# Expert units in pairs over 512 columns, the lower one with its weights straight from the ring

## The reference

```python
g_idx = jnp.argmax(g_logits, axis=-1)                      # 1 of 4 groups
top_vals, top_idx = lax.top_k(e_in, TOP_K)                 # 2 of its 8 experts
for gi in range(N_EXPERT_GROUPS):
    hg = jnp.einsum('nd,edf->nef', xt, w_eg[gi])           # 1024 -> 256, gate
    hu = jnp.einsum('nd,edf->nef', xt, w_eu[gi])           # 1024 -> 256, up
    h = jax.nn.silu(hg) * hu * combine[:, gi, :, None]
    y = y + jnp.einsum('nef,efd->nd', h, w_ed[gi])         # 256 -> 1024, down
```

## Time and profile before

| | us |
|---|---|
| median of 3 runs | 1335.88 |
| lowest, highest | 1333.59, 1340.38 |
| the profiled execution, its own time | 1345.06 |
| its span, first to last instruction | 1343.3 |
| end of the last expert's matmul (start 1284.26 and 2.86) | 1287.1 |

### The profile page before, as it was taken

One profiled execution on the slowest core, in us unless ns is written; L12 is line 12 of the kernel. 1 busy time (PEld: TensorE's weight loads), 2 busy tenths in 40 slices (PEclk: granted clock), 3 DMA queues, 4 the chain that ended last, 5 costly groups with the idle time before them and its releaser, 6 DMA issues.

```text
span 1343.3 us, 25378 instructions
## 1 busy us (share of the span) xinstructions
PE 1166.9 (87%) x9960; PEld 723.4 (54%) x9960; DVE 781.9 (58%) x1330; ACT 381.5 (28%) x668; POOL 257.5 (19%) x321
## 2 busy tenths in 40 slices
PE   4999999999998689999789899953999989999920
PEld 3455555555556578888784455432555545454500
DVE  4277799862314688888733132247555546555546
ACT  4100011011213245555420111111344434443421
POOL 5000000000002223232200000002343434342310
PEclk9899999999999799999969899965999999999965
DMA  7311111010000011110251211073999998775046
GB/s 203 98 32 32 32 39 47 16 37 20 0 0 5 14 21 17 17 17 15 46 171 36 94 63 55 32 281 121 393 383 365 414 423 339 309 289 187 32 185 237
DMA packets 101209, 171.80 MB, mean 128 GB/s; under 512 B 48156, under 2 KB 72595, under 8 KB 91840
## 3 DMA queue, kind: packets, MB, share of 16 engines
q1 hardware_dynamic: 93215, 152.70, 31.8%
q0 software_dynamic: 7904, 17.84, 3.6%
HBM read 153.83 MB, written 26.11 MB: 134 GB/s over the span
## 4 chain that ended last, share of the span: by engine, by line
PE 67%; DVE 12%; DMA 11%; issue 5%; ACT 2%; SPq 1%; POOL 1%; DVEq 1%; POOLq 0%; ACTq 0%
PE ps L1396 26%; PE ps L1700 9%; PE ps L1809 7%; DMA late<-xn_rows,g_idx 6%; PE ps L1423 4%; PE ps L1831 4%; PE ps L1444 2%; DMA arena<-in_w_exp_down_dram 2%; DMA arena<-y_rows 2%; DVE arena L2102 1%; PE ps L1796 1%; PE ps L1728 1%; PE ps L1432 1%; DMA arena<-in_x_prompt_dram 1%; DVE arena L2105 1%
## 5 line engine op out<-in xcount | busy, mean ns | idle before, releaser
L1396 PE MATMUL ps<-arena 128*128 128x512 f32 (+1 forms) x1056 | 348.9, 492 | 0.6 <-ACT arena L881 0.6
L1396 PEld LDWEIGHTS ps<-arena 128*128 128x128 f32 x1056 | 176.3, 193 | 174.4 <-issue 173.6
L1809 PE MATMUL ps<-arena 128*64 128x256 f32 x1664 | 201.8, 385 | 4.9 <-DVE arena L2480 4.9
L1928 DVE SCALAR_TENSOR_TENSOR arena<-arena,cw 128x1024 f32<-128x1024 f32 x240 | 168.2, 778 | 0.4
L1809 PEld LDWEIGHTS ps<-arena 128*64 128x64 f32 x1664 | 117.7, 138 | 85.0 <-issue 35.7
L2480 DVE COPY arena<-arena 128x4096 f32 x52 | 119.5, 2299 | 74.9 <-issue 52.6
L1700 PE MATMUL ps<-arena 128*128 128x512 f32 (+1 forms) x288 | 128.9, 603 | 0.0
L1209 ACT ACTIVATE arena<-arena 128x2048 f32 x52 | 99.4, 1912 | 64.8 <-PE ps L1831 40.9
L1423 PE MATMUL ps<-arena 64*64 64x64 f32 x2864 | 98.9, 222 | 13.8 <-DVE arena L2114 9.8
L1831 PE MATMUL ps<-arena 128*64 128x512 f32 x416 | 103.2, 617 | 8.3 <-DVE arena L2496 5.0
L1423 PEld LDWEIGHTS ps<-arena 64*64 64x64 f32 x2864 | 92.2, 138 | 18.8 <-DVE arena L2114 10.9
(11 more groups left out here) (298 smaller groups left out, 1476.5 us busy)
## 6 DMA issues: line engine op xcount, KB each, us to landing
arena<-in_w_exp_gate_dram SPq DMA_DIRECT2D x32, 1024.0 KB, 8.1
arena<-in_w_exp_up_dram SPq DMA_DIRECT2D x32, 1024.0 KB, 10.8
arena<-in_w_exp_down_dram SPq DMA_DIRECT2D x32, 1024.0 KB, 10.4
arena<-in_w_in_dram SPq DMA_DIRECT2D x22, 512.0 KB, 4.0
arena<-in_x_prompt_dram SPq DMA_DIRECT2D x16, 512.0 KB, 4.2
arena<-y_rows SPq DMA_DIRECT2D x8, 1024.0 KB, 5.8
arena<-in_w_out_dram SPq DMA_DIRECT2D x2, 2048.0 KB, 9.7
xn_rows<-arena SPq DMA_DIRECT2D x8, 512.0 KB, 2.9
```

What stands on the lines that cost most here:

```text
L1396: ins = pe.matmul(pr[:, n0:n1], win[q % 6][:, c, :], xnT[:, c, n0:n1], start=(c == 0), stop=(c == DC - 1))
L1809: ins = pe.matmul(banks(j % 2)[HS * h:HS * h + HS, 0:2 * P], xgT[(j // 2) % 2][:, c, tok], wgu[j % 2][:, :, c, h * P:(h + 1) * P], start=( ...
L1928: dve.scalar_tensor_tensor(out=dst, in0=src, scalar=w, in1=dst, op0=ALU.mult, op1=ALU.add).then_inc(conv_tap, 1)
```

## The change

The loop goes by pairs instead of units. gate_up makes for each chunk two matmuls of 512 columns side by side, the lower 64 rows of the array's output for the lower unit, the upper 64 for the upper one. The lower unit's matmuls read gate, up and down weights from the ring, at an address that PE takes from a register (slot_of); only the upper unit's weights are copied, so DVE and ACT make one weight copy per pair. Sigmoid, products, hidden transposes, their copy and the output copies are made once per pair at twice the width, gathers and scatters once per pair.

SP's loop is reordered. A slot is free for the gate and up weights of e when PE has finished gate_up of the last unit of e-4 (gu_psum, which goes up by two at the end of a pair), and for down weights when the down projection is done (yd_psum, likewise). The arrival of gate and up weights and that of down weights are announced apart (gu_here, wd_here). dve_step(g) issues copy_gate_up(g+2) after the products of pair g+1.

The tables are changed too: counts are rounded to units by arithmetic instead of by comparisons with 16 thresholds, the tables of expert and slot are made with one unit to a partition and turned into a row by PE (two small matmuls), `turns_ready` is set before the row tables are, and the softmax's weights are computed after them.

```diff
--- before.py
+++ after.py
-UT = 4
-HS = P // 2
+NQ = 2
+HS = P // NQ
 RW = 4
 NUNIT = NE + (N * TOPK - NE) // HS
-NUP = -(-NUNIT // UT) * UT
+NUP = -(-NUNIT // (2 * NQ)) * 2 * NQ
+NGR = NUP // NQ
+ROUND = 12582912.0
...
-            def expert_arrived(e):
+            def gate_up_arrived(e):
                 sp.wait_ge(wgu_in[e % RW], wgu_0[e % RW] + 32 * (e // RW + 1))
+                sp.sem_inc(gu_here, 1)
+            def down_arrived(e):
                 sp.wait_ge(wd_in[e % RW], wd_0[e % RW] + 16 * (e // RW + 1))
-                sp.sem_inc(expert_here, 1)
+                sp.sem_inc(wd_here, 1)
+            def units_through(e):
+                return sp.value_load(expert_ends[0:1, e:e + 1], min_val=1, max_val=NUP)
...
-            expert_arrived(0)
+            gate_up_arrived(0)
+            gate_up_arrived(1)
+            down_arrived(0)
             sp.wait_ge(turns_ready, 1)
-            tail_sp = sp.value_load(last_turn[0:1, 0:1], min_val=NE // UT - 2, max_val=NUP // UT - 2)
-            for e in range(RW, NE + 1):
+            tail_sp = sp.value_load(last_turn[0:1, 0:1], min_val=NE // (2 * NQ) - 2, max_val=NGR // 2 - 2)
+            for e in range(RW, NE + 3):
                 if e < NE:
-                    units_done = sp.value_load(expert_ends[0:1, e - RW:e - RW + 1], min_val=1, max_val=NUP)
-                    sp.wait_ge(gu_copied, units_done)
+                    sp.wait_ge(gu_psum, units_through(e - RW))
                     load_gate_up(e)
-                    expert_arrived(e - RW + 1)
-                if e > RW:
-                    units_done = sp.value_load(expert_ends[0:1, e - RW - 1:e - RW], min_val=1, max_val=NUP)
-                    sp.wait_ge(down_copied, units_done)
+                if e - 2 < NE:
+                    gate_up_arrived(e - 2)
+                if RW <= e - 1 < NE:
+                    sp.wait_ge(yd_psum, units_through(e - 1 - RW))
                     load_down(e - 1)
-            for e in range(NE - RW + 1, NE):
-                expert_arrived(e)
-            all_units = tail_sp * UT + 2 * UT
-            scattered = tail_sp * 16 + 32
-            sp.wait_ge(yd_psum, all_units)
+                down_arrived(e - 3)
...
+            def scatter(g, b):
+                pool.wait_ge(ye_act, g + 1)
+                pool.wait_ge(ye_dve, g + 1)
...
+            def pool_step(turn, b, left):
+                g = 2 * turn + b
+                if left >= 4:
+                    pool.wait_ge(xT_psum, 2 * NT + g + 3)
+                    gather(g + 4, b)
+                scatter(g, b)
...
+            def copy_down(g):
+                u = NQ * g + 1
+                need = act.value_load(unit_need[0:1, bass.ds(u, 1)], min_val=1, max_val=NE)
+                slot = act.value_load(unit_slot[0:1, bass.ds(u, 1)], min_val=0, max_val=RW - 1)
+                act.wait_ge(yd_psum, NQ * g)
+                act.wait_ge(wd_here, need)
...
+            def act_step(turn, b, left):
+                g = 2 * turn + b
                 if left >= 1:
-                    sigmoid(u + 1, j + 1)
-                if j % 2 == 0:
-                    if left >= 5:
-                        copy_xg(2 * turn + j // 2 + 2, (j // 2) % 2)
-                    act.wait_ge(yd_psum, u + 1)
-                    act.wait_ge(ye_out[j], 16 * turn)
-                    act.activation(ye[j], banks(5), ACT.Copy).then_inc(ye_act, 1)
+                    sigmoid(g + 1, 1 - b)
+                if left >= 2:
+                    copy_xg(g + 2, b)
+                act.wait_ge(yd_psum, NQ * g + NQ)
+                act.wait_ge(ye_out[b], 16 * turn)
+                act.activation(ye[b][:, 0:512], banks(5), ACT.Copy).then_inc(ye_act, 1)
                 if left >= 1:
-                    copy_down(u + 1)
+                    copy_down(g + 1)
...
+            def slot_of(g):
+                return pe.value_load(unit_slot[0:1, bass.ds(NQ * g, 1)], min_val=0, max_val=RW - 1)
+            def gate_up(g, b, chunks, slot):
                 if 0 in chunks:
-                    if j % 2 == 0:
-                        pe.wait_ge(xT_act, 2 * NT + pair + 1)
-                        pe.wait_ge(xT_dve, 2 * NT + pair + 1)
-                    pe.wait_ge(gu_copied, u + 1)
+                    pe.wait_ge(xT_act, 2 * NT + g + 1)
+                    pe.wait_ge(xT_dve, 2 * NT + g + 1)
+                    pe.wait_ge(gu_copied, g + 1)
                 for c in chunks:
-                    for h in range(2):
-                        ins = pe.matmul(banks(j % 2)[HS * h:HS * h + HS, 0:2 * P], xgT[(j // 2) % 2][:, c, tok],
-                                        wgu[j % 2][:, :, c, h * P:(h + 1) * P], start=(c == 0), stop=(c == DC - 1))
+                    pe.matmul(banks(b)[0:HS, :], xgT[b][:, c, 0:HS],
+                              wring_gu[:, bass.ds(slot, 1), 0:2, c, :].rearrange("p a w f -> p (a w) f"),
+                              start=(c == 0), stop=(c == DC - 1))
+                    ins = pe.matmul(banks(b)[HS:P, :], xgT[b][:, c, HS:P], wgu[b][:, :, c, :], start=(c == 0),
+                                    stop=(c == DC - 1))
                 if DC - 1 in chunks:
-                    ins.then_inc(gu_psum, 1)
-            def pe_step(turn, j, left):
-                u = UT * turn + j
-                next_pair = 2 * turn + (j + 1) // 2
+                    ins.then_inc(gu_psum, NQ)
+            def pe_step(turn, b, left):
+                g = 2 * turn + b
                 if left >= 1:
-                    gate_up(u + 1, next_pair, j + 1, range(0, 5))
-                pe.wait_ge(hx_done, u + 1)
-                pe.transpose(banks(4)[:, (j % 2) * P:(j % 2 + 1) * P], gu, ident[:, :]).then_inc(ht_psum, 1)
+                    slot = slot_of(g + 1)
+                    gate_up(g + 1, 1 - b, range(0, 4), slot)
+                pe.wait_ge(hx_done, g + 1)
+                for c in range(2):
+                    ins = pe.transpose(banks(4)[:, c * P:(c + 1) * P], gu[:, c * P:(c + 1) * P], ident[:, :])
+                ins.then_inc(ht_psum, 1)
                 if left >= 1:
-                    gate_up(u + 1, next_pair, j + 1, range(5, DC))
-                if j % 2 == 0 and left >= 5:
-                    transpose_rows(2 * turn + j // 2 + 2, turn, j // 2 + 2)
-                pe.wait_ge(ht_done, u + 1)
-                pe.wait_ge((ye_act, ye_dve)[j % 2], 2 * turn + j // 2)
-                pe.wait_ge(down_copied, u + 1)
-                for c in range(2):
-                    for h in range(2):
-                        ins = pe.matmul(banks(5 + j % 2)[HS * h:HS * h + HS, :], hT[:, HS * c:HS * c + HS],
-                                        wd[:, c, h * 512:h * 512 + 512], start=(c == 0), stop=(c == 1))
-                ins.then_inc(yd_psum, 1)
+                    gate_up(g + 1, 1 - b, range(4, DC), slot)
+                slot = slot_of(g)
+                if left >= 2:
+                    transpose_rows(g + 2, turn + 1, b)
+                pe.wait_ge(ht_done, g + 1)
+                pe.wait_ge(ye_act, g)
+                pe.wait_ge(ye_dve, g)
+                pe.wait_ge(down_copied, g + 1)
+                for half in range(2):
+                    for c in range(2):
+                        n0 = 2 * DC * F + c * D + half * 512
+                        pe.matmul(banks(5 + half)[0:HS, :], hT[:, c, 0:HS],
+                                  wring[:, bass.ds(slot, 1), n0:n0 + 512].rearrange("p a n -> p (a n)"),
+                                  start=(c == 0), stop=(c == 1))
+                        ins = pe.matmul(banks(5 + half)[HS:P, :], hT[:, c, HS:P], wd[:, c, half * 512:half * 512 + 512],
+                                        start=(c == 0), stop=(c == 1))
+                ins.then_inc(yd_psum, NQ)
...
-            dve.wait_ge(softmax_done, 1)
-            RED(r_pg, r_gd, ALU.add)
-            dve.wait_ge(softmax_done, 2)
-            TS(r_den, r_ex, 1.0, None, ALU.add)
-            TT(r_den, r_den, r_pg, ALU.mult)
-            link(dve.reciprocal(w_k[:, 0, :], r_den))
-            TT(w_k[:, 1, :], w_k[:, 0, :], r_ex, ALU.mult)
...
+            def whole_units(out, v, shift):
+                TS(out, v, 1.0 / HS, shift - 0.5 + 0.5 / HS, ALU.mult, ALU.add)
+                TS(out, out, ROUND, None, ALU.add)
+                TS(out, out, -ROUND, None, ALU.add)
...
+            TS(r_le, upto, r_pid, None, ALU.is_le)
+            RED(r_te, r_le, ALU.add)
+            TS(r_te, r_te, float(NE - 1), None, ALU.min)
+            TS(r_fc, r_thr, r_te, None, ALU.is_le)
+            RED(r_fl, r_fc, ALU.add)
+            link(dve.scalar_tensor_tensor(out=r_col[:, 0:1], in0=r_fl, scalar=-float(RW), in1=r_te, op0=ALU.mult,
+                                          op1=ALU.add))
+            dve.tensor_scalar(r_col[:, 1:2], r_te, 1.0, None, ALU.add).then_inc(cum_done, 1)
...
+                for i in range(NT):
+                    ins = dve.tensor_scalar(r_os[k][:, i, :], r_iots, slot[:, i:i + 1], r_val[:, i:i + 1], ALU.is_equal,
```

(103 more changed lines are left out.)

200 lines of the change are left out of this document (70 added, 130 removed).

## The result

The changed kernel takes **1386.36 us** (median of 4 runs, 1385.35 to 1393.52) against 1337.03 for the kernel before in 4 runs beside it (1333.59 to 1340.38): ratio **1.038**, interval 1.034 to 1.043, slower. The forecast was 1379 in a range of 1346 to 1406. The profiled execution took 1385.48, its span is 1383.7. Between the medians lie 49.3 us where the forecast had 43.

The account below looks back on a forecast made before the run. Bound: DVE's 13.0 us chain against PE's 11.9, plus SP's late announcements. 947.2 + 24 x 13.0 + 36 + 9 x 1.6 = 1309.6; PE ends at 1329, 42 later; scatter 1; 43 on 1335.88 gives 1379 us, range 1346 to 1406.

Parts of the forecast that it names:

- The sign and the mechanism: Loop by pairs: slower, as PE waits for DVE's weight copy and SP's late announcements; 0.85 chance of slower.
- the sum: Whole kernel: PE ends 42 us later, the last scatter adds 1, so 43 us slower.
- PE's stream: PE's own work on a pair: 11.9 us, 0.4 less than before, taken alone worth 10 us.
- Rival 3: PE's wide matmuls save all the rows allow, 0.4 us for each of 26 pairs: 1369 us; chance 0.02.
- DVE's chain: From gate_up through sigmoid, products, row copy, register reads and weight copy to the next gate_up: 13.0 us a cycle.
- The eight long cycles: Pairs 2, 4, 6, 9 to 13: SP's late announcement adds 3.6 us to five, 6.1 to three, 36 in all.
- the clock: PE after 4.7 or 7.2 us idle: lower clock costs 1.4 to 1.9 us a time, 1.6 taken, nine times.
- Tables and start: Before the loop: gate_up(0) starts near 932.0 instead of 939.93, bounds 0 and 10 us gained; gate_up(1) at 947.2.
- 1 (announcements don't hold the copy): SP's announcements don't hold DVE's weight copy, only the 13.0 us cycle is left: 1325 us; chance 0.15.
- 2 (registers on PE): PE pays for its register reads and addresses, 1.0 us in each of 26 pairs: 1405 us; chance 0.12.
- 4 (a quicker SP, or a clock that holds): Long cycles exist but cost less: 1365 us if the clock holds, 1347 with half of the 36 gone; chance 0.11.
- the weights' transfer is hidden: DMA in pairs of one-unit experts: 17.9 us a pair, within cycles of 19.1 and more, so no added time.

Follow-up runs that it names:

- the first experiment: Changed kernel with SP announcing gate and up weights one iteration earlier, before the wait for the down projection: 1350.96 us, ratio 1.009.
- three small edits: In the changed kernel: gate and up announced one iteration earlier, weight copy before the products, down load one iteration later; together 1330.98 us, ratio 0.994.
- the kernel with both orders: Changed kernel with gate and up announced one iteration earlier, DVE's weight copy before the products, down load one iteration later: 1330.98 us, ratio 0.994.

## Why the prediction held, and where it was off

**The sign and the mechanism held.** By positions of the two profiled executions: the part ahead of the tables -7.3 (no part of the change), tables -9.8, from gate_up(0) to PE's end 1326.7 - 922.8 = 403.9 against 347.2, +56.7, and behind it +0.8: sum 40.4, as their own times differ. Without the first it is 47.7 where the sum said 43. The 4.7 are the balance of misses both ways: from gate_up(1) to gate_up(25) it is 369.9 instead of 362.4, +7.5; the tables -1.9; from gate_up(0) to gate_up(1) +0.4; from gate_up(25) to PE's end 18.4 instead of 19.5, -1.1; the last scatter -0.2.

**PE's stream.** Forecast 11.9, measured 12.0 where nothing disturbs it. Rival 3 needed it shorter still. 0.34 a pair is gained, no more than the rows' 0.4. The Trainium skill, "TensorEngine Tiling (Array Packing)", section Instruction Overhead, gives each matmul some 60 cycles of overhead. Added to every matmul, which is how the prediction made its estimate from that page, it would have the stream 0.8 shorter than the forecast, 11.1; the trace, with 12.0, disagrees. The prediction's use of it had a fault of its own: the 0.214 us for 512 columns was measured, so any overhead is in the 11.9 already. The section adds that a matmul of one column takes as long as one of 60; read as such a floor it says nothing of 256 or 512 columns, and no run here tests it.

**DVE's chain.** 13.0 forecast, 12.83 to 13.13 measured. Its interpolated steps were right: sigmoid of 256 columns 0.384 (0.38), products 0.424 (0.42). That it is the bound is shown by the copy's place: ahead of the products the cycle is 12.0.

**The eight long cycles** are those named, pairs 2, 4, 6, 9 to 13. They sum to 160.2 us where the forecast has 5 x 18.2 + 3 x 20.7 = 153.1. The idle times ahead of the eight gate_ups were right (46.2 in all against 45.1). The term that was most **mis-sized is the clock**: from gate_up to the hidden transposes they take 4.97 to 6.58 us instead of 3.58, 2.0 more on average where the step said 1.6, at most 3.0 where it said 1.9; that is 3.5 of the 7.1 us. Another 2.5 is PE's step, 12.2 in this kernel without idle time and clock, where 11.9 was taken; the last 1.1 is the idle time.

**Tables and start.** 9.8 gained, 7.9 forecast, both within the bounds. gate_up(1) starts 15.6 after gate_up(0), 15.2 forecast; the announcement for it did come with the second SP iteration (934.38), but the products and the row copy end it, as the step had them in this order.

**Rivals.** 1 (announcements don't hold the copy) fell with the first experiment, and its price was near: that kernel's three long cycles hold 57.5 - 3 x 13.0 = 18.5 us, and without them it would be at 1332, where the rival said 1325. 2 (registers on PE) is refuted for the reads by the doubled reads; matmuls with a register address can cost no more than the 0.1 between the 11.9, put together from rows without one, and the 12.0 measured. 4 (a quicker SP, or a clock that holds) went the other way. That the weights' transfer is hidden is shown for the changed kernel, by half of their bytes and by SP's rows; once SP's order is mended it is hidden no longer.

The clock wasn't tried by itself: no edit was found that leaves PE idle and keeps its clock.

## What to carry over

When a copy that ran ahead becomes the last thing before its consumer, write down the new ring (consumer, producer's queue, consumer) and sum it: where it is longer than the consumer's own work it is the new cycle, however much work the change saves. Follow each announcement back through the queue that makes it: here a wait for the consumer's own last step stood one or two iterations ahead of it, and with the queue's order on DVE this cost 55 us, which three small edits gave back. What that queue itself waited for tells order from rate: 120.5 us for the consumer's last step and none for a DMA here, 4.3 and 98 after the edits. And order a queue so that what may be late stands behind what is ready, unless it is never late.

## What the hardware showed that was not expected

- The same idle time cost PE quite different amounts afterwards: behind 4.6 to 4.9 us idle the first half of gate_up took 4.97, 5.04, 5.20, 5.28 and 6.43 us (3.58 at the upper level), behind 7.4 to 7.8 us idle 5.27, 6.22 and 6.58.
- PE's reads of a register cost nothing that could be measured (ratio 0.9945 with 51 more reads, 0.9936 without), where two reads on DVE show as 0.83 to 0.95 us of idle time ahead of its copy. Matmuls whose address comes from a register (L1815) take as long as those beside them with a fixed one (L1818): 209.1 and 209.2 us for 416 records each.
- The copy of 4096 columns took 2.29 us in some ordinary cycles of the changed kernel and 2.47 to 2.55 in others. With 0.11 more idle time ahead of the copies of 2.47, and none ahead of those of 2.55, this makes cycles of 12.83 and of 13.1. In the kernel with both orders it is 2.29 to 2.32 in all of them. Why was not tried.
